# FFN head: third block's products ahead of the row means, low products of the first two behind them, and later waits in the down blocks

## What is computed

```python
def rmsnorm_2(x, gain):
    xf = x.astype(jnp.float32)
    y = xf * lax.rsqrt(jnp.mean(xf * xf, axis=-1, keepdims=True) + EPS)
    return (y * gain.astype(jnp.float32)).astype(x.dtype)

def swiglu(x, w_gu, w_down):
    g, u = jnp.split(x @ w_gu, 2, axis=-1)
    return (jax.nn.silu(g) * u) @ w_down

    for layer in range(DEPTH_2):                      # 4
        g = norm_gains[layer]
        h = x + 0.5 * swiglu(rmsnorm_2(x, g[0]), w_ffn_gu[layer, 0], w_ffn_down[layer, 0])
        xn = rmsnorm_2(h, g[1])
...
        h = h + 0.5 * swiglu(rmsnorm_2(h, g[2]), w_ffn_gu[layer, 1], w_ffn_down[layer, 1])
        gate = jax.nn.sigmoid(rmsnorm_2(h, g[3]) @ w_ple_gate[layer])
        x = h + gate * (p[layer] @ w_ple_proj[layer])
```

## Time and profile before

| | us |
|---|---|
| median of 3 runs | 2399.87 |
| the profiled execution | 2407.7 |
| span of its instructions | 2405.7 |
| PE busy | 2392.4 (99%) |
| DVE busy | 1727.9 (72%) |
| ACT busy | 1342.0 (56%) |
| matmuls on PE | 20328 |
| weight blocks loaded | 781, median 4.0 us from issue to landing |

### The profile page before, as it was taken

The page is one execution under the profiler, slowest core; times in us unless marked ns, Lnnn a source line. Parts: engine busy times, 40 slices in busy tenths (PEclk is TensorE's granted clock), DMA queues, the critical chain, the costliest instruction groups (busy, mean ns, idle before and its releaser), DMA issues.

```text
span 2405.7 us, 51567 instructions
## 1 busy us (share of the span) xinstructions
PE 2392.4 (99%) x20328; PEld 2362.4 (98%) x20328; DVE 1727.9 (72%) x2431; ACT 1342.0 (56%) x2044; POOL 78.8 (3%) x77
## 2 busy tenths in 40 slices
PE   9999999999999999999999999999999999999999
PEld 9999999999999999999999999999999999999999
DVE  8879867668776677667766686688667766877666
ACT  5756655447564465445644564467446644766444
POOL 1000000001100000000000000000000000220000
PEclk9999999999999999999999999999999999999999
DMA  7325326555355556555465565644655655535653
GB/s 269 115 64 174 123 80 226 185 184 162 128 187 190 197 170 211 190 184 185 140 202 197 171 210 191 196 137 137 202 188 183 202 195 189 166 124 192 196 196 125
DMA packets 115377, 418.85 MB, mean 174 GB/s; under 512 B 12832, under 2 KB 14112, under 8 KB 114976
## 3 DMA queue, kind: packets, MB, share of 16 engines
q1 hardware_dynamic: 114096, 412.40, 52.3%
q0 software_dynamic: 560, 2.10, 0.3%
q10 hardware_dynamic: 576, 2.27, 0.3%
HBM read 414.62 MB, written 2.10 MB: 173 GB/s over the span
## 4 chain that ended last, share of the span: by engine, by line
PE 94%; DVE 3%; ACT 2%; DMA 1%; issue 1%; POOL 0%; ACTq 0%; SPq 0%; DVEq 0%
PE ps_gu L140 17%; PE ps_gu L146 17%; PE ps_gu L141 17%; PE ps_acc L140 9%; PE ps_acc L146 8%; PE ps_acc L141 8%; PE ps_acc L2744 1%; PE ps_acc L2302 1%; DVE w_lo L100 1%; PE ps_misc L140 1%; PE ps_gu L2338 1%; PE ps_misc L146 1%; PE ps_misc L141 1%; PE ps_sum L140 1%; PE ps_sum L146 1%; PE ps_sum L141 1%
## 5 line engine op out<-in xcount | busy, mean ns | idle before, releaser
L100 DVE TENSOR_TENSOR w_lo<-w_raw,w_hi 128x1024 fp32r<-128x1024 f32 x781 | 953.6, 1227 | 367.3 <-ACT w_hi L92 359.5
L140 PE MATMUL ps_gu<-xn_hi,w_hi 128*128 128x256 f32 x3832 | 1051.6, 279 | 1.2 <-DVE w_lo L100 0.5
L141 PE MATMUL ps_gu<-xn_hi,w_lo 128*128 128x256 f32 x3832 | 1042.7, 276 | 0.0
L92 ACT ACTIVATE w_hi<-w_raw 128x1024 fp32r<-128x1024 f32 x781 | 820.2, 1056 | 368.2 <-PE ps_gu L146 270.3
L146 PE MATMUL ps_gu<-xn_lo,w_hi 128*128 128x256 f32 x3832 | 1001.2, 277 | 0.0
L140 PEld LDWEIGHTS ps_gu<-xn_hi,w_hi 128*128 128x128 f32 x3832 | 719.2, 188 | 4.1 <-issue 2.0
L141 PEld LDWEIGHTS ps_gu<-xn_hi,w_lo 128*128 128x128 f32 x3832 | 719.4, 188 | 0.4
L146 PEld LDWEIGHTS ps_gu<-xn_lo,w_hi 128*128 128x128 f32 x3832 | 692.9, 188 | 0.2
L140 PE MATMUL ps_acc<-h_hi,w_hi 128*128 128x256 f32 x1496 | 415.5, 278 | 0.2 <-DVE h_lo L576 0.2
L146 PE MATMUL ps_acc<-h_lo,w_hi 128*128 128x256 f32 x1496 | 413.6, 276 | 0.0
L141 PE MATMUL ps_acc<-h_hi,w_lo 128*128 128x256 f32 x1496 | 413.5, 276 | 0.0
(11 more groups left out here) (479 smaller groups left out, 2573.4 us busy)
## 6 DMA issues: line engine op xcount, KB each, us to landing
w_raw<-in_w_dram SPq DMA_DIRECT2D x781, 512.0 KB, 4.0
const<-in_const_dram SPq DMA_DIRECT2D x1, 1216.0 KB, 8.5
distance_rows<-arena POOLq DMA_DIRECT2D x1, 1024.0 KB, 7.8
p_all<-distance_rows POOLq DMA_DIRECT2D x2, 512.0 KB, 5.3
p_all<-in_p_dram ACTq DMA_DIRECT2D x1, 1024.0 KB, 6.0
out_dram<-x_res SPq DMA_DIRECT2D x8, 128.0 KB, 1.9
x_res<-in_x_dram ACTq DMA_DIRECT2D x1, 512.0 KB, 6.6
x_res<-in_x_dram SPq DMA_DIRECT2D x1, 512.0 KB, 6.0
```

The source lines that it names most:

```text
L92: act.activation(self.w_hi[:, s, :], self.w_raw[:, r, :], ACT.Copy).then_inc(self.w_hi_ready.sem, 1)
L100: dve.tensor_tensor(self.w_lo[:, s, :], self.w_raw[:, c % NR, :], self.w_hi[:, s, :], ALU.subtract)\
L140: pe.matmul(out, self.w_hi[:, s, j0:j0 + width], rhs_hi, start=start, stop=False, skip_group_check=True)
L141: pe.matmul(out, self.w_lo[:, s, j0:j0 + width], rhs_hi, start=False, stop=False, skip_group_check=True)
```

## The change

The order of `first()`: high products of blocks 0 and 1 for all j; then block 2, for each j its high products and its low one; the sums; then the low products of blocks 0 and 1. The semaphore chunk_done, which counts blocks in order, rises by one and then by two at the end of that, so that block 2 counts as done when 0 and 1 are. `down` waits for h_hi at its start and for h_lo before its third matmul. The splits of weight blocks move to other places: behind a PLE stage block 2's low part goes ahead of the folds; block 6's two parts go behind h_hi and h_lo of tile 0 in every FFN (behind a PLE stage they stood there already, with block 5's low part); in the first FFN the low parts of blocks 3 and 4, which stood between and behind the folds, go behind the folds and behind the scale of tile 0, and block 5's goes behind h_lo.

```diff
--- before.py
+++ after.py
@@ -453,12 +453,14 @@
     @block.tensor
     def _(pe):
         def down(t, c, i):
-            pe.wait_ge(*hl.at(b0 + t + 1 + STEP * i))
+            pe.wait_ge(*hh.at(b0 + t + 1 + STEP * i))
             k.wait_chunk(pe, c, i)
             for m in range(KD):
-                mm = k.products(pe, k.ps_acc[:, m // 2, (m % 2) * S:(m % 2 + 1) * S], c % NS, m * P, P,
-                                k.h_hi[:, t % 2, :], k.h_lo[:, t % 2, :], False, t == FT - 1,
-                                start=(t == 0 and m % 2 == 0))
+                out = k.ps_acc[:, m // 2, (m % 2) * S:(m % 2 + 1) * S]
+                k.with_hi(pe, out, c % NS, m * P, P, k.h_hi[:, t % 2, :], t == 0 and m % 2 == 0)
+                if m == 0:
+                    pe.wait_ge(*hl.at(b0 + t + 1 + STEP * i))
+                mm = k.with_lo(pe, out, c % NS, m * P, P, k.h_lo[:, t % 2, :], t == FT - 1)
                 if t == FT - 1 and m % 2 and m < KD - 1:
                     mm.then_inc(k("acc_bank_done").sem, 1)
             mm.then_inc(k.chunk_done.sem, 1)
@@ -479,35 +481,40 @@
                 for n in range(2):
                     mm = k.with_lo(pe, halves[n], (c0 + n) % NS, j * P, P, k.xn_lo[:, j, :], j == KD - 1)
                     if j == KD - 1:
-                        mm.then_inc(k.chunk_done.sem, 1)
-            for j in range(KD - 1):
+                        mm.then_inc(k.chunk_done.sem, 1 + n)
+            next_out = k.ps_gu[1][:, 0:S]
+
+            def begin_next():
+                pe.wait_ge(*free[1])
+                k.wait_chunk(pe, c0 + 2)
+
+            def next_high(j):
+                k.with_hi(pe, next_out, (c0 + 2) % NS, j * P, P, k.xn_hi[:, j, :], j == 0)
+
+            for j in range(KD):
                 high(j)
-            for j in range(KD - 2):
+            begin_next()
+            for j in range(KD):
+                next_high(j)
+                pe.wait_ge(*lo_at[j])
+                k.with_lo(pe, next_out, (c0 + 2) % NS, j * P, P, k.xn_lo[:, j, :], False)
+            sum_rows(k, pe, k.norms, k.summed)
+            for j in range(KD):
                 low(j)
-            high(KD - 1)
-            low(KD - 2)
-            low(KD - 1)
-            sum_rows(k, pe, k.norms, k.summed)
 
         def tile(t, i):
             if t == 0:
                 return first()
-            if t == 1:
-                pe.wait_ge(*free[1])
             if t >= 2:
                 pe.wait_ge(*hr.at(b0 + t - 1 + STEP * i))
             for n, c in enumerate((at_g(t), at_g(t) + 1)):
+                if t == 1 and n == 0:
+                    continue
                 k.wait_chunk(pe, c, i)
-                out = k.ps_gu[t % 2][:, n * S:(n + 1) * S]
-                if t == 1 and n == 0:
-                    for j in range(KD):
-                        k.with_hi(pe, out, c % NS, j * P, P, k.xn_hi[:, j, :], j == 0)
-                    for j in range(KD):
-                        mm = k.with_lo(pe, out, c % NS, j * P, P, k.xn_lo[:, j, :], j == KD - 1)
-                else:
-                    for j in range(KD):
-                        mm = k.products(pe, out, c % NS, j * P, P, k.xn_hi[:, j, :], k.xn_lo[:, j, :], False, j == KD - 1,
-                                        start=(n == 0 and j == 0))
+                for j in range(KD):
+                    mm = k.products(pe, k.ps_gu[t % 2][:, n * S:(n + 1) * S], c % NS, j * P, P,
+                                    k.xn_hi[:, j, :], k.xn_lo[:, j, :], False, j == KD - 1,
+                                    start=(n == 0 and j == 0))
                 mm.then_inc(k.chunk_done.sem, 1)
             down(t - 1, at_g(t) + 2, i)
 
@@ -521,10 +528,9 @@
                 for c in late[0]:
                     k.hi(act, c)
             k.hi(act, g + AHEAD, i)
-            behind = t == 0 and late[1]
             if t == 0:
                 act.preload_act_table_set("natural_log_exp_and_others")
-            if not behind:
+            else:
                 k.hi(act, g + 1 + AHEAD, i)
             if t == 0:
                 root_rows(k, act)
@@ -537,7 +543,7 @@
                 k.hi(act, g + 2 + AHEAD, i)
             act.wait_ge(*hr.at(b0 + t + 1 + STEP * i))
             act.activation(k.h_hi[:, t % 2, :], k.h[:, t % 2, :], ACT.Copy).then_inc(hh.sem, 1)
-            if behind:
+            if t == 0:
                 k.hi(act, g + 1 + AHEAD, i)
             if t == FT - 1:
                 k.hi(act, g + 2 + AHEAD)
@@ -552,19 +558,21 @@
                 for c in late[1]:
                     k.lo(dve, c)
             behind = t == 0 and late[1]
-            if t == 0 and k.inner:
-                k.inner.outer(dve)
-            if not behind:
+            inner = k.inner if t == 0 else None
+            if inner:
+                k.lo(dve, g + 3)
+                inner.outer(dve)
+            elif not behind:
                 k.lo(dve, g + AHEAD, i)
-                if not (t == 0 and k.inner):
+                if t:
                     k.lo(dve, g + 1 + AHEAD, i)
             if t == 0:
                 dve.wait_ge(*k("rstd_ready").at(k.norms))
             dve.wait_ge(k.chunk_done.sem, g + 2 + i * TURN)
             gu = k.ps_gu[t % 2][:, :].rearrange("p (n t) -> p n t", n=2)
             dve.tensor_tensor(gu, gu, k.rstd[:, :].unsqueeze(1).to_broadcast([P, 2, S]), ALU.mult).then_inc(sc.sem, 1)
-            if t == 0 and k.inner:
-                k.lo(dve, g + 1 + AHEAD, i)
+            if inner:
+                k.lo(dve, g + 4)
             dve.wait_ge(*silu.at(b0 + t + 1 + STEP * i))
             if t >= 2:
                 dve.wait_ge(*hl.at(b0 + t - 1 + STEP * i))
@@ -575,8 +583,9 @@
             dve.wait_ge(*hh.at(b0 + t + 1 + STEP * i))
             dve.tensor_tensor(k.h_lo[:, t % 2, :], k.h[:, t % 2, :], k.h_hi[:, t % 2, :], ALU.subtract)\
                .then_inc(hl.sem, 1)
-            if behind:
+            if behind or inner:
                 k.lo(dve, g + AHEAD, i)
+            if t == 0:
                 k.lo(dve, g + 1 + AHEAD, i)
             if t == 2 and k.inner:
                 k.inner.to_x(dve)
@@ -730,12 +739,13 @@
             dve.tensor_tensor(k.x[:, m, :], k.x[:, m, :], k.h[:, m % 2, :], ALU.add).then_inc(xr.sem, 1)
         if nxt:
             nxt.split_lo(dve, KD - 2)
+            k.lo(dve, to_ffn[0])
             nxt.fold_step(dve, 0)
             nxt.split_lo(dve, KD - 1)
             nxt.fold_step(dve, 1)
             nxt.fold_step(dve, 2)
 
-    k.late = to_ffn[2:], to_ffn
+    k.late = to_ffn[2:], to_ffn[1:]
     k.x_at = after
     k.used += 2 + KD
     k.p_read = c0 + 2
@@ -1366,11 +1376,13 @@
                     nxt.fold_step(dve, 0)
                 if t == KD - 1 and inner:
                     inner.fold_step(dve, 0)
-            k.lo_for(dve, c0 + KD - 2)
+            if not inner:
+                k.lo_for(dve, c0 + KD - 2)
             fold(dve, 1)
             nxt.split_lo(dve, KD - 1)
             fold(dve, 2)
-            k.lo_for(dve, c0 + KD - 1)
+            if not inner:
+                k.lo_for(dve, c0 + KD - 1)
 
         k.used += KD
         k.x_at = at
```

## The result

The changed kernel takes 2427.63 us (median of 10 runs, 2415.45 to 2433.01) against 2400.32 for the kernel before beside it (10 runs, 2398.66 to 2416.93): a ratio of 1.0096, 95% interval 1.0072 to 1.012. It is slower, by 17 to 29 us by that interval; the medians are 27 us apart. The prediction, 2397.2 in a range of 2388 to 2408, was wrong in the size and in the direction. The profiled execution took 2431.2 us (span 2429.4), where the one of before took 2407.7: 23.5 more.

A forecast was written before the change was run, and what follows sets the result against it. TensorE (PE), busy 99% of the span, was taken as the bound. Terms +0.1 + 0.1 - 0.6 - 0.9 - 1.4 = -2.7 us took the profiled 2407.7 to 2405.0, or 2397.2 from the runs' median 2399.87; range 2388 to 2408.

The forecast's parts named there:

- Step 3: DVE's and ACT's moved splits: behind PLE stages block 2's w_lo 0.03 late with the restart, in three FFNs, +0.1 us.
- Step 5: Down blocks' waits: stalls at seven FFNs' ends go, -0.9 us, and slow pace behind them, -1.4; met waits cost nothing.
- rival C: A thin margin at down blocks is missing, putting FFNs on the slow pace, +8.2 us each: 2405 to 2422; chance 0.18.
- Step 1: Order in first(): nothing stalls in seven ordinary heads, so no gain; restart behind the sums costs 7 x 0.01, +0.1 us.
- Step 2: First down blocks, tile 0: old wait would stall PE 0.1; new waits leave a 0.03 us margin, cost 0 us.
- Step 3, tile 1: Three FFNs behind PLE: tile 1's h_lo later, N + 10.9 to 11.2, wanted at N + 11.00; no stall taken, other end 0.2.
- Step 4: First FFN's head: wait for inner squares goes, h_lo 0.36 earlier, PE stalls for h_hi; -0.6 us, between -0.2 and -0.9.
- rival A: The forecast itself, 2397.2 (2395.5 to 2399): first FFN stays slow, still stalling at its first down block; chance 0.48.
- Rival D: Each down block's added wait costs what a restart does, 0.05: 176 x 0.05 = 9 us, 2406; chance 0.03.
- Rival B: First FFN gets the fast pace: 1488 matmuls x 5.5 ns = 8.2 us, 2389.0; chance 0.24.

The follow-up runs named there:

- e3: Changed kernel with block 2's w_lo ahead of xn_lo of tile 6 on DVE in the PLE stages; 2401.65 us, ratio to the kernel before 1.0003.
- e14: Changed kernel with block 2 of each head issuing its 16 high products first, in pairs, then its 8 low ones; 2413.33 us.
- e1: Changed kernel; in the four heads with four sum matmuls, half of block 2 and 12 low products before the sums, eight high products in pairs behind; 2406.26 us.
- e4: Kernel before with only the down blocks' new waits (h_hi at the head, h_lo at the third matmul); 2418.52 us.
- e8: e4 with block 2's w_lo ahead of xn_lo of tile 6 in the PLE stages; 2424.45 us.
- e7: Changed kernel with the down blocks' old waits (one wait for h_lo at the head); 2447.61 us.
- e5: e3 with the first FFN's first down block issued as 16 high products in pairs, then 8 low ones; 2412.91 us.
- e6: e5 with e1's order around the sums of the four heads with four sum matmuls; 2406.3 us.
- e9: Changed kernel; in every tile's second up block the first four steps issue only high products in pairs, their low ones last; 2397.42 us, ratio to before 0.9948.
- e13: e7 with the block order of e9; 2403.28 us.
- e2: Changed kernel without the sum over the means' second tile in the three heads behind PLE, so two fp32 matmuls instead of four; 2426.74 us.

## Why the prediction was wrong
**Step 3 failed, at its first term.** It found the late w_lo of block 2 in the three heads behind PLE: 0.03 late with the restart in each, +0.1 us for all three. The matmul that waits for it is 0.02 late, and the one behind it 0.08 more, so the stall itself takes 0.10 in each head, 0.3 in all. The earlier trace rows had shown that second part, and Step 5 counts it; Step 3 left it out. That is the small error. The large one is that the stall was priced at its length. What stood behind it was 24.4 us in the profile, three FFNs on the slow pace. The prediction's own rows had shown that a stall of this size can leave the slow pace behind, and rival C had priced that at 8.2 for an FFN, 2422 for three (the median came to 2427.6); C looked for it only at the down blocks, where I had a margin, and not at the place where I had a stall. e3 takes the stall away, and the median falls by 26 us.

**Step 1** priced the restart behind the sums at 0.01 for each of seven heads, and 0.02 to 0.06 is measured. Over the last 100 starts up to the first down block the heads behind a mixer take 11.61 us where they took 11.59, and in e3, with the new order and no stall, those behind PLE take 11.82 where they took 11.76 to 11.79. Its premise that nothing stalls in these heads was not so behind PLE: the kernel before has its late w_lo there, with no time to show for it. What the step left out is that the old order had 16 pairs behind that late w_lo and the new one has threes, then low products alone. In e14 and e1, with pairs at either place, the six profiled heads come out of the stall fast; e4 and e8 show that this isn't sure.

**Step 2** held. The changed kernel shows no wait of PE at the first down blocks of the seven ordinary FFNs, and e7 shows the stall that the old wait makes there, 0.08 where I had 0.1, with another 0.11 at the next matmul that I hadn't, and 8.2 behind it in four FFNs. The margin of 0.03, small as it is, was enough in every profile with both the new waits and the new order.

**Step 3, tile 1**: "the loads should come in time" did not hold in the third FFN. The wait for h_lo made a start come 0.33 behind the one before it instead of 0.12, at 920.83; ACT's h_hi and DVE's h_lo stood behind the splits of a block that landed at 918.1. In the changed kernel this FFN was slow already, so it cost 0.3; in e14, e5 and e6 it cost the pace.

**Step 4** came out in its time, but mostly for another reason. The wait for the inner squares is gone, and the first low down product starts at 375.73 where it started at 376.18:

```profile
376.18 0.28 PE L146 MATMUL ps_acc<-h_lo,w_hi 128*128 128x256 f32 x1
```

That is -0.45, or -0.52 from the head's first fold (361.50 here, 361.43 before), for a forecast of -0.6, within -0.2 and -0.9. PE stalls for h_hi, as said:

```profile
375.27 0.39 PE L140 MATMUL ps_acc<-h_hi,w_hi 128*128 128x256 f32 x1 [0.26 <-ACT h_hi L545]
375.50 0.28 PE L141 MATMUL ps_acc<-h_hi,w_lo 128*128 128x256 f32 x1
375.73 0.39 PE L146 MATMUL ps_acc<-h_lo,w_hi 128*128 128x256 f32 x1
```

But h_lo was to come 0.36 earlier, and it comes 0.11 earlier than in the earlier trace rows, 0.17 from the first fold:

```profile
375.25 0.43 DVE L584 TENSOR_TENSOR h_lo<-h,h_hi 128x256 fp32r<-128x256 f32 x1 [0.48 <-ACT h_hi L545]
```

(In the profiles of the other kernels with these splits it is 0.17 to 0.39.) The last sum starts at 369.89 where the step had 369.65. e4, which has the new waits and none of the moved splits, already starts that product 14.40 us behind its first fold, where it was 14.75 before and is 14.23 in the changed kernel. So 0.35 of the 0.52 is the new waits in `down`, and 0.17 the moved splits:

```profile
375.77 0.39 PE L146 MATMUL ps_acc<-h_lo,w_hi 128*128 128x256 f32 x1
```

The FFN stays slow, as said, but not because of the stall at its down block, as rival A had it. Its starts are 0.119 apart from the sums on, as at 372.35 and 372.47. So here the forecast held by another cause than the one it named, which is luck. In e1, where the first FFN comes to that stall at 0.113 and leaves it slow, the named cause is the one at work.

**Step 5** was right in sum: no wait at the end of any FFN, and 73 matmuls in 8 us behind the fourth's, where the earlier trace rows had 69 at its place.

```profile
1375.50:1383.50 8.00, 8.00 (x73) 1.00 0.22 74
```

Up to the 100th matmul behind their end the down streams of FFNs 2, 4, 6 and 8 are 0.15, 0.58, 0.15 and 0.57 shorter, and e4's span gives -2.05 against -2.3, or some -1.7 without the first FFN's part. Rival D, 0.05 for each added wait, is out: 1414 in 160 us as before, with one more wait in each of 176 down blocks. What the Trainium skill (Advanced Engine Details and Errata, Miscellaneous Facts) gives for a sequencer's reading of a semaphore, 50 to 100 ns, didn't appear on PE's path in this stream.

**Rival B** had the wrong level. The first FFN on the fast pace gives 2397.4 (e9, all windows fast, profile and runs alike), and no run of any kernel here came near 2389. The 7.8 us by which the profile of before lay above its runs were one slow FFN that most of those runs didn't have, as the case against B had it. So the forecast's own number, 2397.2, is what the kernel would take with all FFNs on the fast pace: e3's lowest five runs are 2397.0 to 2398.7.

Against rival C I had set that seven FFNs run alike, 1414 or 1415 each. That was one profile, in which none of them had a stall ahead of threes; it told how even the fast pace is, not how safe it is.

## What to carry to other kernels
Where the trace shows two paces for the same stream of matmuls at the same granted clock, price a wait by what stands behind it up to the next thing that ends the slow pace, not by its length; and ask it of the stalls that you forecast before the margins that you doubt. Look for an order of the same matmuls that ends the slow pace from inside the stream (here some high products in pairs on one moving operand in every tile): in the five kernels that have it, e9 to e13, the runs of each lie within 1.0 to 3.9 us, and none of the 32 is a step of 8.2 up. It was worth more than any single stall removed. When runs of one kernel lie on levels, find what one level is before reading a profile as typical.

## What the runs showed of the hardware
Matmuls of 256 columns in threes (two on one moving operand, one on the next) run in this kernel at 113.2 or at 118.7 ns from start to start, both at a granted clock of 1.00, and either lasts for some 1500 matmuls if nothing intervenes. The Trainium skill (TensorE: Matmul & The Clock Gate, Back-to-back issue gap) gives N/2.4 + 2.5 for the isolated gap of a warm matmul, for 256 columns an estimated 109. For a stream with weight loads it has figures at 128 and 512 columns, 81 and 131 ns, and none at 256. The rows show two paces at 256, and neither is 109.

What moved PE between them here. A matmul that starts 0.01 to 1.0 us late for a semaphore, with 0.08 to 0.11 more at the matmul behind it, can set the slow pace. The 16 low products behind the sums run at 0.118 in any case; what comes behind them is at 0.113 again if PE was there before the sums (all 33 such places of e3, e5 and e14 outside the first FFN, PLE stages among them) and slow if it was slow before them (all six of the changed kernel and e2). In the first FFN, whose last sum is another line, PE is at 0.113 before the sums and slow behind them in all of these. Pairs in the stream left no FFN slow in e9 to e13; a slow stretch lasted there at most some 10 us (e13, 1192.0 to 1202.3). Which way a single wait goes isn't settled by its length: 0.19 and 0.12 led back to the fast pace in the kernel before and not in e4, and the same starts 0.18 apart led back to it in e7's third FFN and not in its fifth. What in PE holds the pace, no run shows.
